# First expert's slot list formed on chip; its rows gathered, turned and split in the routing block

## The reference

```
x = x + matmul(mixed, w_out);  h = rms_norm(x, g_ffn)
logits = h @ w_router + b_router
top_logit, top_idx = top_k(logits, 4)          # of 32 experts
gates = softmax(top_logit)
for each chosen (token, expert):
    gate, lin = split(h @ w_gate_up[e] + b_gate_up[e])       # 1024 -> 2 x 1024
    gate, lin = min(gate, 7), clip(lin, -7, 7)
    y += gates * (((lin + 1) * gate * sigmoid(1.702 * gate)) @ w_down[e] + b_down[e])
out = rms_norm(x + y, g_final)
```

## Time and profile before

| | |
|---|---|
| median of three runs | 2507.99 us |
| the profiled execution | 2506.09 us |
| its span, first to last instruction | 2504.5 us |
| PE busy | 2425.9 us (97%) |
| PEld, DVE, ACT busy | 1958.6, 1496.6, 1223.8 us |
| POOL busy | 368.8 us |
| DMA | 537.08 MB, mean 214 GB/s |
| mean granted TensorE clock | 0.988 |

### The profile page before, as it was taken

How to read it: one execution, slowest core, us unless ns; L and a number is a source line. 1 busy time by engine, 2 the same in 40 slices (tenths; PEclk the granted TensorE clock), 3 DMA queues, 4 the chain that set the end, 5 groups by cost and what they waited for, 6 DMA issues and landing times.

```text
span 2504.5 us, 41446 instructions
## 1 busy us (share of the span) xinstructions
PE 2425.9 (97%) x14271; PEld 1958.6 (78%) x14272; DVE 1496.6 (60%) x1483; ACT 1223.8 (49%) x1256; POOL 368.8 (15%) x384
## 2 busy tenths in 40 slices
PE   7999999999999999995999999999999999999997
PEld 6987777898888877994778777777777787777775
DVE  4311333332333324335789888788877898788977
ACT  6412344321111111144667766676756776667766
POOL 0000000000000000434112121212112211212120
PEclk9999999999999999997999999999999999999998
DMA  4134233323422222535899997999989998989998
GB/s 132 35 40 62 68 68 72 59 48 51 51 51 51 92 93 81 183 124 183 292 365 381 337 348 280 345 342 346 336 285 316 377 379 307 324 303 380 350 338 304
DMA packets 262381, 537.08 MB, mean 214 GB/s; under 512 B 28984, under 2 KB 79928, under 8 KB 261184
## 3 DMA queue, kind: packets, MB, share of 16 engines
q1 hardware_dynamic: 241280, 489.35, 58.9%
q0 software_dynamic: 21024, 46.65, 6.8%
HBM read 493.32 MB, written 42.63 MB: 214 GB/s over the span
## 4 chain that ended last, share of the span: by engine, by line
PE 51%; DVE 1%; issue 0%; ACT 0%; DMA 0%; POOL 0%; POOLq 0%; DVEq 0%; ACTq 0%
PE m_gate L2171 5%; PE m_gate L2167 5%; PE m_lin L2167 5%; PE m_gate L2169 5%; PE m_lin L2171 5%; PE m_lin L2169 5%; PE m_y L2167 5%; PE m_y L2171 5%; PE m_y L2169 5%; PE m_spill L2208 3%; PE m_spill L2220 2%; PE m_turn L2159 1%; PE m_gate L2177 1%; PE m_gate L2145 1%; PE m_lin L2145 1%; PE m_y L2177 1%
## 5 line engine op out<-in xcount | busy, mean ns | idle before, releaser
L1982 DVE TENSOR_TENSOR m_w_lo<-raw,m_w_hi 128x2048 fp32r<-128x2048 f32 x384 | 871.4, 2287 | 208.9 <-ACT m_w_hi L1851 207.2
L1851 ACT CAST m_w_hi<-raw 128x2048 fp32r<-128x2048 f32 x384 | 734.5, 1914 | 356.8 <-PE m_lin L2171 251.4
L107 PE MATMUL c_bank<-h_hi_r,ring_hi 128*128 128x512 f32 x640 | 252.2, 394 | 0.9 <-PEq L397 0.9
L109 PE MATMUL c_bank<-h_lo_r,ring_hi 128*128 128x512 f32 x640 | 249.7, 390 | 0.0
L110 PE MATMUL c_bank<-h_hi_r,ring_raw_r 128*128 128x512 f32 x640 | 249.4, 390 | 0.0
L148 ACT CAST ring_hi<-ring_raw 128x2048 fp32r<-128x2048 f32 x43 | 82.0, 1908 | 306.6 <-DMA ring_raw<-in_w_in 133.6
L2167 PE MATMUL m_gate<-m_w_hi,m_x_hi 128*128 128x512 f32 x512 | 218.1, 426 | 0.0
L2167 PE MATMUL m_y<-m_w_hi,m_a_hi 128*128 128x512 f32 x512 | 211.0, 412 | 1.8 <-DVE m_a_lo L2034 1.8
L2171 PE MATMUL m_gate<-m_w_hi,m_x_lo 128*128 128x512 f32 x512 | 200.8, 392 | 0.0
L2167 PE MATMUL m_lin<-m_w_hi,m_x_hi 128*128 128x512 f32 x512 | 200.4, 391 | 0.0
L2171 PE MATMUL m_y<-m_w_hi,m_a_lo 128*128 128x512 f32 x512 | 200.4, 391 | 0.0
(11 more groups left out here) (337 smaller groups left out, 4501.7 us busy)
## 6 DMA issues: line engine op xcount, KB each, us to landing
raw<-in_w_gate_up SPq DMA_DIRECT2D x512, 512.0 KB, 11.4
raw<-in_w_down SPq DMA_DIRECT2D x256, 512.0 KB, 12.5
ring_raw<-in_w_in SPq DMA_DIRECT2D x31, 1024.0 KB, 10.1
gates<-work POOLq DMA_DIRECT2D x32, 256.0 KB, 2.6
work<-gates SPq DMA_DIRECT2D x8, 1024.0 KB, 6.8
v<-in_x SPq DMA_DIRECT2D x8, 512.0 KB, 11.3
ring_raw<-in_w_branch_b SPq DMA_DIRECT2D x4, 1024.0 KB, 5.0
ring_raw<-in_w_branch_a SPq DMA_DIRECT2D x4, 1024.0 KB, 5.0
```

Source lines behind the costliest of these rows:

```text
L107: pe.matmul(out, left_hi(k), right_hi(k), start=first and k == kts[0], stop=False, skip_group_check=True)
L109: pe.matmul(out, left_hi(k), right_lo(k), start=False, stop=False, skip_group_check=True)
L1851: act.copy(w_hi[:, p % WS].rearrange("p k b n -> p (k b n)"), raw[:, raw_slot(m)].rearrange("p k b n -> p (k b n)")).then_inc(signals.whi, 1)
L1982: dve.tensor_tensor(w_lo[:, p % WS].rearrange("p k b n -> p (k b n)"), raw[:, raw_slot(m)].rearrange("p k b n -> p (k b n)"), f32(w_hi[:, ...
```

## The change

While the tiles are routed, DVE compares each token's seat at expert 0 with the numbers 1 to 128 (and 129 to 160, four times over), which gives one-hot matrices g_sel; PE multiplies them with the tokens' row numbers (g_row_b) and sums over the tiles, and DVE writes the sums to slot_in. So the first list isn't read back from DRAM. Its rows are gathered by POOL inside the routing block, before the last tile's four scatters; PE turns them into `turned[0]`, and ACT and DVE split them into x_hi and x_lo there. ACT also splits panels 0 and 1 there (high parts, in memory that the trace calls v_r), DVE the low part of panel 0. SP's order at the block's end is another: panels 2 and 3 ahead of the sixth store of h_rows (counted from 0), panels 4 and 5 ahead of the seventh. SP waits for POOL's scatters in POOL's stead. The bias buffer shares memory with g_ht, so the first `norm` waits for the bias split. The first two panels' products in the expert block read the new split buffers; the register loads of DVE and PE come behind them.

```diff
+        b_raw = ht[:, :, :].rearrange("p s d -> p (s d)")
...
                 sp.dma_start(y_rows[i * P:(i + 1) * P, :], x2[:, i]).then_inc(finished, 16)
+                if i == TT - 1:
+                    for m in range(2, 4):
+                        load_panel(sp, w_gate_up, w_down, raw, signals.raw_loaded, m, 0)
+                if i >= TT - 2:
+                    continue
                 sp.wait_ge(normed, i + 1)
                 sp.dma_start(h_rows[i * P:(i + 1) * P, :], ht[:, i % HT]).then_inc(stored[i % HT], 16)
-            for m in range(2, 4):
-                load_panel(sp, w_gate_up, w_down, raw, signals.raw_loaded, m, 0)
+            for i in range(TT - 2, TT):
+                sp.wait_ge(normed, i + 1)
+                sp.dma_start(h_rows[i * P:(i + 1) * P, :], ht[:, i % HT]).then_inc(stored[i % HT], 16)
+                if i == TT - 2:
+                    for m in range(4, 6):
+                        load_panel(sp, w_gate_up, w_down, raw, signals.raw_loaded, m, 0)
             sp.wait_ge(finished, 16 * (TT + 2))
+            sp.wait_ge(sent, 16 * TT * TOP_K)
...
             pool.wait_ge(cleared, 16 * E * ROOM // (P * P))
             for i in range(TT):
+                if i == TT - 1:
+                    pool.wait_ge(first_listed, 2)
+                    for s in range(HT):
+                        pool.wait_ge(stored[s], 16 * len(range(s, TT, HT)))
+                    pool.indirect_dma_start(out=xg[:, :], out_offset=None, in_=h_rows[:, :],
+                                            in_offset=bass.IndirectOffsetOnAxis(ap=slot_in[:, 0, 0:1], axis=0)) \
+                        .then_inc(signals.gathered[0], 16)
+                    pool.indirect_dma_start(out=xs_g[:, :], out_offset=None,
+                                            in_=h_rows.rearrange("r (g c) -> (r g) c", g=NG),
+                                            in_offset=bass.IndirectOffsetOnAxis(ap=slot_in[:, 1, 0:1], axis=0)) \
+                        .then_inc(signals.first_spill, 16)
                 pool.wait_ge(slotted, i + 1)
                 for k in range(TOP_K):
                     pool.indirect_dma_start(out=slot_rows[:, :],
                                             out_offset=bass.IndirectOffsetOnAxis(ap=place[:, i, k:k + 1], axis=0),
                                             in_=slots[:, i, k, :], in_offset=None).then_inc(sent, 16)
-            pool.wait_ge(sent, 16 * TT * TOP_K)
-            for s in range(HT):
-                pool.wait_ge(stored[s], 16 * len(range(s, TT, HT)))
-            pool.wait_ge(finished, 16 * (TT + 2))
...
+            act.wait_ge(ready, 4 * TT)
+            for m in range(2):
+                act.wait_ge(signals.raw_loaded[raw_slot(m)], OPEN + 32)
+                act.copy(m_hi[:, 4 * m:4 * m + 2].rearrange("p k n -> p (k n)"),
+                         raw[:, raw_slot(m)].rearrange("p k b n -> p (k b n)")).then_inc(signals.whi, 1)
+            for r in range(2):
+                act.wait_ge(signals.x_turned, OPEN + r + 1)
+                act.copy(x_hi[:, 4 * r:4 * r + 4].rearrange("p k c -> p (k c)"),
+                         turned[0][:, 512 * r:512 * r + 512]).then_inc(signals.xhi, 1)
...
+                if i == 0:
+                    dve.wait_ge(biased, 1)
...
+            def select(i):
+
+                dve.wait_ge(ranked, i + 1)
+                dve.scalar_tensor_tensor(out=key[:, i:i + 1], in0=p_rank[:, E * i:E * i + 1], scalar=1.0,
+                                         in1=chosen[:, i, 0:1], op0=ALU.add, op1=ALU.mult).then_inc(keyed, 1)
+                dve.wait_ge(keyed, i + 1)
+                dve.tensor_scalar(sel[:, i, 0], cst["iota"][:, :], 1.0, key[:, i:i + 1], ALU.add, ALU.is_equal)
+                dve.tensor_scalar(sel[:, i, 1].rearrange("p (g c) -> p g c", g=NG),
+                                  cst["iota"][:, 0:SPILL].unsqueeze(1).to_broadcast([P, NG, SPILL]), 1.0 + P,
+                                  key[:, i:i + 1], ALU.add, ALU.is_equal).then_inc(selected, 1)
+
+            def list_first():
+
+                dve.wait_ge(first_summed, 1)
+                dve.tensor_scalar(slot_in[:, 0, 0:1], p_out[:, 0:1], p_out[:, 1:2], None, ALU.add) \
+                    .then_inc(first_listed, 1)
+                dve.tensor_scalar(slot_in[:, 1, 0:1], p_out[:, 2:3], p_out[:, 3:4], quarter_f[:, :], ALU.add, ALU.add) \
+                    .then_inc(first_listed, 1)
...
+            norm(TT - 1)
+            select(TT - 1)
             seats(TT - 1)
-            norm(TT - 1)
-
-            dve.wait_ge(constant, 1)
+            list_first()
+
+            dve.wait_ge(signals.whi, OPEN + 1)
+            dve.tensor_tensor(m_hi[:, 2:4].rearrange("p k n -> p (k n)"),
+                              raw[:, raw_slot(0)].rearrange("p k b n -> p (k b n)"),
+                              f32(m_hi[:, 0:2].rearrange("p k n -> p (k n)")), ALU.subtract).then_inc(signals.wlo, 1)
...
+            for r in range(2):
+                dve.wait_ge(signals.xhi, OPEN + r + 1)
+                dve.tensor_tensor(x_lo[:, 4 * r:4 * r + 4].rearrange("p k c -> p (k c)"),
+                                  turned[0][:, 512 * r:512 * r + 512],
+                                  f32(x_hi[:, 4 * r:4 * r + 4].rearrange("p k c -> p (k c)")),
+                                  ALU.subtract).then_inc(signals.xlo, 1)
...
+            def first_rows(i):
+                pe.wait_ge(selected, i + 1)
+                for a in range(2):
+                    mm = pe.matmul(p_out[:, 2 * a:2 * a + 2], sel[:, i, a], row_b[:, i, a], start=i == 0 and a == 0,
+                                   stop=i == TT - 1, skip_group_check=True)
+                if i == TT - 1:
+                    mm.then_inc(first_summed, 1)
...
+            for i in range(TT - 1):
+                first_rows(i)
             rank(TT - 1)
+            first_rows(TT - 1)
...
+            pe.wait_ge(signals.gathered[0], 16)
+            for k in range(KT):
+                tr = pe.transpose(turned[0][:, k * P:(k + 1) * P], xg[:, k * P:(k + 1) * P], cst["ident"][:, :])
+                if k % 4 == 3:
+                    tr.then_inc(signals.x_turned, 1)
...
-            sp.wait_ge(signals.gathered[0], 16)
-            sp.wait_ge(signals.first_spill, 16)
-            for m in range(4, MP):
+            for m in range(6, GU):
+                load_panel(sp, w_gate_up, w_down, raw, signals.raw_loaded, m, 0)
+            sp.wait_ge(signals.panel_done, OPEN + 2)
+            for m in range(GU, MP):
...
-            pool.wait_ge(signals.in_listed[0], 16)
-            pool.indirect_dma_start(out=xg[:, :], out_offset=None, in_=h_rows[:, :],
-                                    in_offset=bass.IndirectOffsetOnAxis(ap=slot_in[:, 0, 0:1], axis=0)) \
-                .then_inc(signals.gathered[0], 16)
-            for g in range(NG):
-                pool.dma_start(slot_in[SPILL * g:SPILL * (g + 1), 1, :],
-                               slot_rows[P:P + SPILL, 2 + 2 * g:4 + 2 * g]).then_inc(spill_listed, 16)
-            pool.wait_ge(spill_listed, 16 * NG)
-            pool.indirect_dma_start(out=xs_g[:, :], out_offset=None, in_=h_quarters,
-                                    in_offset=bass.IndirectOffsetOnAxis(ap=slot_in[:, 1, 0:1], axis=0)) \
-                .then_inc(signals.first_spill, 16)
             pool.wait_ge(signals.gathered[0], 16)
             pool.sem_inc(signals.rows_in, 1)
             pool.wait_ge(signals.first_spill, 16)
...
-            for m in range(2):
-                split(m, m + 6, 0)
-            for r in range(2):
-                x_split(r, 0)
             for m in range(2, 4):
-                split(m, m + 6, 0)
+                split(m, m, 0)
             act.wait_ge(signals.whi, OPEN + 4)
             act.sem_inc(signals.whi, 2)
+            for p in range(2):
+                split(4 + p, p, 0)
             act.wait_ge(signals.panel_done, OPEN + 3)
-            split(4, 0, 0)
             sigmoid(0, 0)
+            split(6, 2, 0)
             act.wait_ge(signals.panel_done, OPEN + 4)
...
             pick_expert(0, 0, signals.picked_gu)
-            for m in range(2):
-                split(m, m + 6, OPEN + m + 1)
-            for r in range(2):
-                x_split(r, 0)
+            dve.wait_ge(signals.whi, OPEN + 2)
+            dve.tensor_tensor(w_first[:, 6:8].rearrange("p k n -> p (k n)"),
+                              raw[:, raw_slot(1)].rearrange("p k b n -> p (k b n)"),
+                              f32(w_first[:, 4:6].rearrange("p k n -> p (k n)")), ALU.subtract).then_inc(signals.wlo, 1)
+            last = last_super(dve)
+            held = registers(dve)
             for m in range(2, 4):
-                split(m, m + 6, OPEN + m + 1)
+                split(m, m, OPEN + m + 1)
...
-            x_turn(0)
-            first_second = about(pe, held, 0)[0]
             pe.wait_ge(signals.picked_gu, OPEN + 1)
             pe.wait_ge(signals.xlo, OPEN + 2)
-            for m in range(4):
```

(60 more changed lines are left out.)

38 lines of the change are left out of this document (21 added, 17 removed).

## The result

The kernel after takes 2513.86 us (median of 10 runs, 2512.44 to 2515.34), the kernel before 2508.09 us beside it (10 runs, 2505.26 to 2509.87): ratio 1.0024, with a 95% interval of 1.0016 to 1.0033. So it is slower by 5.8 us, where 5.7 us less were forecast, and outside the range. The profiled execution took 2513.68 us, its span 2512.0 us.

A forecast was written before the change was run, and what follows sets the result against it. PE was taken to bound the expert block, idle at its start; first product 5.4 us earlier plus 0.3 us of waits gave 5.7 us less, median 2507.99 to 2502.3 us, 8-in-10 range 2496.5 to 2508.0 us (own range 2500.3 to 2504.3).

The forecast's parts named there:

- a microsecond gained or lost at its start should come out at the end unchanged: Expert block: PE sets the pace by itself, so a gain at its start reaches the end in full.
- slower: SP's queue at the block's end stays at 186 GB/s, first product 7.3 us late, 2515.3 us; chance 0.06.
- The lead given back in the first expert: PE waits in panels 2 to 11 by as much as was won, 2507.5 us; chance 0.12.
- The last store: Seventh h_rows store on SP's queue: issued at about 1149.4, landing at 1159.0 behind the panel loads.
- From there to the barrier: POOL's gathers and scatters take 7.5 us, last wait to barrier 3.0 us: barrier at 1169.5.
- The rival that the drain could be longer: POOL's drain counts only once scatters have landed, barrier later still, gain about 3 us, 2505.0 us; chance 0.22.
- Barrier to the first product: First bias product 0.5 us behind the barrier, at 1170.0 instead of 1175.40.
- Clock: Behind the first product: 5.2 us at 1.2 GHz again, costing 2.6 us as before, 1.5 us to either side.
- Waits in the first expert: PE's 0.7 us wait for the activation may go; 0.3 us counted as gain.
- The loop over the tiles: Routing loop keeps its time per tile; `select`'s roughly 0.75 us hides in DVE's idle time.
- The largest term, 5.4 us: First bias product in the expert block at 1170.0 instead of 1175.4, so 5.4 us earlier.

The follow-up runs named there:

- after_aligned: The changed kernel with 640 bytes of padding between b_split and x_hi; 2503.24 us against 2508.41 us of the kernel before, ratio 0.9979.
- late45: The changed kernel with the loads of panels 4 and 5 behind the last store of h_rows; 2509.98 us, ratio to the kernel before 1.0007.
- late_all: after_aligned with the loads of panels 2 to 5 behind the last store of h_rows; 2499.32 us against 2507.71 us of the kernel before, ratio 0.9964.
- rel64: The kernel before with 64 bytes of padding ahead of x and a; 2527.30 us in one run.

## Why the prediction was wrong

- **The step that failed: "a microsecond gained or lost at its start should come out at the end unchanged."** It rests on every product of the loop keeping its pace, and I priced the new x_hi and x_lo at nothing. Their distance to the weights went from 0 to 128 bytes (mod 256), and the loop takes 10.9 us more. -5.3 and +10.9 make +5.6 us; measured are +5.8 us. With that distance mended (after_aligned) the median is 5.2 us under before, within 1 us of the forecast and inside its own range. Part of that nearness is luck, as the terms below show.
- **The rival "slower"** named the right sign by a mechanism that did not happen: the store landed at 1162.1 (1159.8 with the 2.3 us taken off), short of the 1164.4 from which it would decide. "The lead given back in the first expert" by waits didn't happen either; it was given back over the whole loop, without waits.
- **The last store.** Forecast: issued at 1149.4, landed at 1159.0. Found: issued at 1151.38, landed at 1162.1, which are 1149.1 and 1159.8 with the 2.3 us taken off; so 10.7 us behind its issue instead of 9.6. The queue took the loads first, as said; the sum was 1.1 us short. One reading in it was wrong: it gave the last of the four halves before the median landing of 7.4 us, but that half's own was the longest, 8.3 us. It landed at 1161.1, so two panels took 8.0 us, not 7.1. In after, panels 2 and 3 had landed at 1153.9, 1151.6 with the 2.3 us off, where the sum has 1150.6.
- **From there to the barrier**: 10.5 us forecast, 1173.4 - 1162.1 = 11.3 found. POOL went on 0.9 us behind the landing instead of 0.2 (also in late45 and late_all). The rest was right: two gathers and four scatters in 7.35 us, then 3.0 us. The rival that the drain could be longer fell for this order of the queue; beside loads (late_all) it holds.
- **Barrier to the first product**: 0.5 us forecast, 0.45 found (1173.85 - 1173.4). So the first product came 3.8 us earlier instead of 5.4; of the 1.6 us that are missing, 0.8 are the store's and 0.7 POOL's going on.
- **Clock**: I expected 5.2 us at the lower level again, with 1.5 us to either side. The windows of after (length, PE, PEld, DVE, ACT, POOL busy, granted clock, DMA share, GB/s) show the rise at 1177.0:

```profile
1175.00:1176.00 1.00, 1.00 (x4) 0.71 (x4) 1.00 (x1) 1.00 (x1) 0.00 (x0) 0.50 0.23 25
1176.00:1177.00 1.00, 1.00 (x4) 0.81 (x3) 0.21 (x2) 1.00 (x2) 0.65 (x2) 0.51 0.93 266
1177.00:1178.00 1.00, 1.00 (x6) 0.82 (x5) 1.00 (x1) 1.00 (x1) 0.97 (x2) 1.00 0.95 274
```

  So 3.1 us at 1.2 GHz (from 1173.85) instead of 5.2: 1.0 us won that I hadn't counted, inside the bound that I gave. In late45 the clock rose 4.0 us behind the first product, in after_aligned 5.8 us (near 1179.6): it varies, and what it gave after is luck.
- **Waits in the first expert**: the 1.1 us for the activation became 0.4; 0.3 forecast, 0.7 found. The loop over the tiles kept its pace: the reciprocal's idle time, 1.04 us, is 0.45 us, which is where `select` went.
- So the 5.3 us are 3.8 (first product), 1.0 (clock) and 0.7 (waits), which make 5.5; the remaining 0.2 us isn't traced. In after_aligned's profile the same terms, with its own drift of 1.7 us, are 3.3, -0.3 and 0.7, and the first turn comes 3.8 us earlier. The largest term, 5.4 us, was thus worth 3.3 to 3.8 us.

## What to carry to other kernels

When a change gives a matmul operand another home, compare its address with that of its partner, modulo 256 bytes, before and after: here each of the four distances tried that is not a multiple of 256 cost 2 to 3% of each product, in a loop that was 97% busy before and after and showed no wait. A steady drift that no wait explains is found by the first and last start of one repeated instruction, and then by the mean of each group of the bounding engine; a busy total misleads where records are missing, so the counts are compared first. And a store that others wait for goes ahead of bulk loads in the same queue: 2.7 us instead of 10.7 us here.

## What the runs showed that I had not expected

- A float32r product of 512 columns took 227 ns from start to start when loaded and streaming operands lay a multiple of 256 bytes apart in the partition (eight kernels here), and 232 to 234 ns when they lay 32, 64, 96 or 128 bytes off it; all in all up to 20 us of 2508 (rel64: loop 1298.9 against 1278.9 us).
- POOL's drain behind indirect transfers ended 2.8 us after the last one's issue had ended with the loads done, and 6.4 us after it beside 4 MB of loads.
- An indirect gather of 128 rows landed in 4.2 us with the loads done, and in 7.1 to 7.8 us beside them.
